# Three narrow products or one wide and one narrow: the up projection of an encoder block at near-fp32 precision

## Chip, cores and metric

The kernel runs on one NeuronCore of a Trainium2 chip. Times are device microseconds (us) of one execution. TensorE is called PE, VectorE DVE, ScalarE ACT, GpSimd POOL; SP, ACT and POOL issue the transfers (DMAs).

## What is computed

One layer of an encoder on x (512 tokens, width 2048), all in float32: RMS norm, one wide input projection feeding pooling, a short convolution and sparse attention, gates, output projection, residual. The change is in the last part, the MLP:

```python
h2 = _rmsnorm(x, norm2[l])
f = jnp.square(jax.nn.relu(jnp.einsum('bsd,df->bsf', h2, w_ff1[l])))   # 2048 -> 8192, the up stage
x = x + jnp.einsum('bsf,fd->bsd', f, w_ff2[l])                          # 8192 -> 2048, the down stage
```

## The kernel before

**Numbers.** Each float32 operand is split in a high part (type fp32r, rounded by ACT's copy) and a low part (DVE subtracts the high part from the source). A product is high x high + high x low + low x high, three passes of PE that add up in PSUM.

**Seven products.** The large matrix products are cut in two along all three dimensions and done by a scheme of seven half-size products with sums of blocks (Strassen's, in Winograd's form). The blocks of a weight are b11, b12, b21, b22; its mixes b11 + b12, b11 + b12 + b22, b12 + b22 and the sum of all four are made on DVE (`mix1`); the operand's seven parts, high and low, lie ready in `sf[h][n]` for the whole stage. The seven products n = 0 to 6 are summed into four result blocks C11, C12, C21, C22.

**The up stage.** `w_ff1` is worked through in 16 pairs (q = 0 to 15), each of 2 x 256 output columns. A pair has 14 granules: product n, half h of the contraction, in the order k = 2n + h (in pair 0 another order, `FIRST_PAIR`). A granule (`f1_granule`, L1261 on) is 4 contraction tiles j times 2 blocks m of 128 weight columns, and for each three products of 256 columns (256 tokens; the two token halves are blocks of the scheme):

```python
pe.matmul(part, hi_at(8, k)[:, cols], sh, start=first, ...)   # L1304
pe.matmul(part, hi_at(8, k)[:, cols], sl, start=False, ...)   # L1305
mm = pe.matmul(part, lo_at(8, k)[:, cols], sh, ...)           # L1306
```

One PSUM bank of 512 columns holds both m. The weight blocks are the stationary operand. ACT makes the high part of granule k (`hi1`, L1750) once granule k-4 is done, DVE the low part (`lo1`, L2612); four buffers each (`f_wh`, `f_wl`) go round. So both engines work about three granules ahead of PE, each strictly in the order in which its instructions are written: after granule k's part come that k's extras (`act_after`, `dve_after`):

- DVE, eight mixes a pair (`mix1`, L2593 to L2606, 1024 columns each), three sums of a bank with a kept copy (`add_c`, L2644 to L2648, 512 columns), and for the pair before four mixes (`mix_s`, L2656 to L2666) and seven low parts (`lo_s`, L2676) of the squared result, which the down stage will use;
- ACT, three copies of a bank (`keep`, L1769), relu and square of four blocks (`square_f`, L1783, L1785), seven high parts (`hi_s`, L1799).

Products that belong to several result blocks run in one PSUM bank as a chain, and the running sum is copied out (`keep`) before the next product is added. PE waits before h = 0 of a product for whatever last read its bank. SP loads four weight blocks a pair in two halves of 512 KB (`load_f1`) and stores the seven pieces in `f_dram` (`spill_f`), all in one queue in program order.

**Other stages.** Phases J = 0 to 5 (gates), 6 and 7 (output projection) and 8 to 15 (down stage) use products of 512 columns (L1200 to L1202). Early in the kernel POOL's queue makes tables of block sums for J = 0, 6, 7 and pair 0 in DRAM (`t_dram`): it copies a block from DRAM to DRAM and adds a second by a transfer with `accum_op`.

## Time and profile before

| | |
|---|---|
| median of 3 runs | 2651.47 us (2651.34 to 2654.2) |
| the profiled execution, its own time | 2653.83 us |
| its span, first to last instruction | 2652.0 us |
| mean granted PE clock | 0.999 of 2.4 GHz |
| busy in the span | PE 99%, PE weight loads 85%, DVE 74%, ACT 47%, POOL 4% |
| DMA over the span | 568.65 MB, mean 214 GB/s |
| up stage, products L1304 to L1306 | from 1381.4 to 2035 us |

How to read it: matmuls are pipelined and their ends are modelled, so a busy PE is not a PE at its peak, and distances between starts tell more than durations. A wait for several semaphores is put down to the one that came last. Idle time of an engine that is not the bottleneck costs nothing.

### The profile page before, as it was taken

Reading aid. Unit: us, or ns where it says so; the run is one execution under the profiler, and the core shown is the slowest. Engines: PE = TensorE matmul, PEld = TensorE weight load, DVE = VectorE, ACT = ScalarE, POOL = GpSimd, SP = SyncE. Lnnn points to the kernel's source line nnn. Section 1 sums busy time; section 2 is a strip of 40 time slices with the busy share of each in tenths; the row PEclk is TensorE's granted clock in tenths of the full one; section 3 lists DMA queues with packets and bytes.
Section 4 is the critical chain, followed back from the end, with each engine's and each line's share of the span. In section 5 each row is a group of like instructions: output and inputs, shape, how many; then the busy total and the mean of one; then the engine's idle time right before and its main releaser. Section 6 shows DMA issues by size and latency. Waiting matters only on the chain.

```text
span 2652.0 us, 36176 instructions
## 1 busy us (share of the span) xinstructions
PE 2628.2 (99%) x14130; PEld 2259.0 (85%) x14130; DVE 1953.9 (74%) x2352; ACT 1241.9 (47%) x1614; POOL 94.4 (4%) x116
## 2 busy tenths in 40 slices
PE   8999999999999999999999999999999999999999
PEld 6688877777888888888889999999999788888887
DVE  4565645567777775567668888888887988888887
ACT  6322343335444543234556656656655433333333
POOL 0022222100000000000000000000000000000000
PEclk9999999999999999999999999999999999999999
DMA  7589999946455547556764566565568777685753
GB/s 240 175 227 246 256 257 239 258 137 242 160 181 175 173 162 266 176 174 211 257 231 140 187 215 197 176 223 176 198 223 306 274 262 261 214 317 178 273 190 122
DMA packets 316804, 568.65 MB, mean 214 GB/s; under 512 B 20000, under 2 KB 128160, under 8 KB 316128
## 3 DMA queue, kind: packets, MB, share of 16 engines
q1 hardware_dynamic: 272976, 434.16, 48.5%
q0 software_dynamic: 20736, 58.73, 9.8%
q10 hardware_dynamic: 22928, 73.54, 7.5%
q8 instruction: 107, 1.75, 0.3%
q14 instruction: 57, 0.47, 0.1%
HBM read 473.95 MB, written 150.99 MB: 236 GB/s over the span
## 4 chain that ended last, share of the span: by engine, by line
PE 93%; DVE 3%; DMA 2%; issue 1%; ACT 1%; SPq 0%; ACTq 0%; DVEq 0%
PE aux L1200 8%; PE aux L1201 8%; PE aux L1202 8%; PE main L1304 8%; PE main L1306 8%; PE main L1305 8%; PE main L1200 6%; PE main L1201 6%; PE main L1202 6%; PE main L513 5%; PE main L515 5%; PE main L514 5%; PE main L1045 1%; PE main L1235 1%; PE aux L1235 1%; PE main L1047 1%
## 5 line engine op out<-in xcount | busy, mean ns | idle before, releaser
L1304 PE MATMUL main<-sf,f_wh 128*128 128x256 f32 x1728 | 489.2, 283 | 1.7 <-DVE cf_low L2737 1.4
L1305 PE MATMUL main<-sf,f_wh 128*128 128x256 f32 x1728 | 489.0, 283 | 0.0
L1306 PE MATMUL main<-sf,f_wl 128*128 128x256 f32 x1728 | 489.0, 283 | 0.0
L1304 PEld LDWEIGHTS main<-sf,f_wh 128*128 128x128 f32 x1728 | 331.8, 192 | 2.1 <-DVE cf_low L2737 1.6
L1305 PEld LDWEIGHTS main<-sf,f_wh 128*128 128x128 f32 x1728 | 331.8, 192 | 0.0
L1306 PEld LDWEIGHTS main<-sf,f_wl 128*128 128x128 f32 x1728 | 331.8, 192 | 0.0
L488 DVE TENSOR_TENSOR w_lo<-w_raw,w_hi 128x512 fp32r<-128x512 f32 (+1 forms) x184 | 123.3, 674 | 209.8 <-ACT w_hi L481 208.8
L481 ACT ACTIVATE w_hi<-w_raw 128x512 fp32r<-128x512 f32 (+1 forms) x184 | 113.4, 617 | 276.4 <-PE main L515 212.1
L513 PE MATMUL main<-act_hi,w_hi 128*128 128x512 f32 x576 | 229.7, 399 | 8.5 <-DVE w_lo L488 7.6
L1471 ACT ACTIVATE f_wh<-group 128x1024 fp32r<-128x1024 f32 x128 | 135.7, 1061 | 200.0 <-PE aux L1202 105.5
L515 PE MATMUL main<-act_hi,w_lo 128*128 128x512 f32 x576 | 225.6, 392 | 0.0
L514 PE MATMUL main<-act_lo,w_hi 128*128 128x512 f32 x576 | 225.3, 391 | 0.0
L2612 DVE TENSOR_TENSOR f_wl<-f1raw,f_wh 128x1024 fp32r<-128x1024 f32 x130 | 158.3, 1219 | 64.7 <-ACT f_wh L1750 64.7
L2149 DVE TENSOR_TENSOR f_wl<-group,f_wh 128x1024 fp32r<-128x1024 f32 x128 | 156.3, 1221 | 66.5 <-ACT f_wh L1471 66.5
L1200 PE MATMUL aux<-f_wh,sf 128*128 128x512 f32 x512 | 199.3, 389 | 2.4 <-DVE yb L2767 2.4
L1202 PE MATMUL aux<-f_wh,sf 128*128 128x512 f32 x512 | 199.2, 389 | 0.0
L1201 PE MATMUL aux<-f_wl,sf 128*128 128x512 f32 x512 | 199.2, 389 | 0.0
L1750 ACT ACTIVATE f_wh<-f1raw 128x1024 fp32r<-128x1024 f32 x130 | 136.9, 1055 | 86.2 <-PE main L1306 79.9
L1471 ACT ACTIVATE f_wh<-f2x 128x1024 fp32r<-128x1024 f32 x96 | 102.0, 1062 | 151.8 <-PE aux L1202 80.1
L2149 DVE TENSOR_TENSOR g_wl<-group_g,g_wh 128x1024 fp32r<-128x1024 f32 x80 | 97.9, 1224 | 72.8 <-ACT g_wh L1471 72.8
L1200 PE MATMUL main<-f_wh,sf 128*128 128x512 f32 x384 | 149.5, 389 | 0.5 <-DVE yb L2769 0.5
L1201 PE MATMUL main<-f_wl,sf 128*128 128x512 f32 x384 | 149.4, 389 | 0.0
(311 smaller groups left out, 5910.1 us busy)
## 6 DMA issues: line engine op xcount, KB each, us to landing
group<-w_ff SPq DMA_DIRECT2D x160, 512.0 KB, 5.1
f1raw<-w_ff SPq DMA_DIRECT2D x126, 512.0 KB, 5.6
sf<-f_dram ACTq DMA_DIRECT2D x56, 1024.0 KB, 11.2
group_g<-w_in SPq DMA_DIRECT2D x100, 512.0 KB, 4.4
w_raw<-w_in SPq DMA_DIRECT2D x87, 512.0 KB, 8.7
f_dram<-piece_hi SPq DMA_DIRECT2D x112, 256.0 KB, 4.0
f_dram<-piece_lo SPq DMA_DIRECT2D x112, 256.0 KB, 5.0
t_dram<-w_o POOLq DMA_DIRECT2D x48, 512.0 KB, 8.6
```

The source lines that it names most:

```text
L513: pe.matmul(out, wh, hi[:, kt, :], start=(kt == last_kt[0]), stop=False)
L514: pe.matmul(out, wh, lo[:, kt, :], start=False, stop=False)
L515: mm = pe.matmul(out, wl, hi[:, kt, :], start=False, stop=(kt == last_kt[1]))
L1200: pe.matmul(part, sh, wh, start=first, stop=False, skip_group_check=True)
L1201: pe.matmul(part, sh, wl, start=False, stop=False, skip_group_check=True)
L1202: mm = pe.matmul(part, sl, wh, start=False, stop=last, skip_group_check=True)
L1304: pe.matmul(part, hi_at(8, k)[:, cols], sh, start=first, stop=False, skip_group_check=True)
L1305: pe.matmul(part, hi_at(8, k)[:, cols], sl, start=False, stop=False, skip_group_check=True)
L1306: mm = pe.matmul(part, lo_at(8, k)[:, cols], sh, start=False, stop=last, skip_group_check=True)
L1471: act.activation(hi_at(J, k_of(J, n, g))[:], source_of(J, n, g).rearrange("p k c -> p (k c)"), ACT.Copy).then_inc(f_hi, 1)
L2149: dve.tensor_tensor(lo_at(J, k)[:], source_of(J, n, g).rearrange("p k c -> p (k c)"), hi_at(J, k)[:].bitcast(F32), ALU.subtract).then_inc( ...
L2612: dve.tensor_tensor(lo_at(8, k)[:], f1_source(q, n, h).rearrange("p k c -> p (k c)"), hi_at(8, k)[:].bitcast(F32), ALU.subtract).then_inc( ...
```

## The change

**Products.** In pairs 1 to 15 the high weight block is multiplied with both parts of the operand at once: a product of 512 columns, [high part | low part], into a whole bank, so that high x high lies in columns 0 to 255 and high x low in columns 256 to 511. The third product (low weight, high operand part) has 256 columns and adds to the first half. Each m has its own bank, so a product takes two banks. Pair 0 stays as it was (`f1_first`).

```diff
-                bank = main[:, (q % 2, 2, q % 2, 2, q % 2, 3, q % 2)[n], :]
+                banks = aux[:, 0:2, :] if n in (1, 3) else aux[:, 2:4, :] if n == 5 else chain_banks(q)
...
                 for j in range(4):
-                    sh, sl = sf[h][n][:, 0, j, :], sf[h][n][:, 1, j, :]
+                    both, sh = sf[h][n][:, :, j, :], sf[h][n][:, 0, j, :]
                     for m in range(2):
...
-                        pe.matmul(part, hi_at(8, k)[:, cols], sh, start=first, stop=False, skip_group_check=True)
-                        pe.matmul(part, hi_at(8, k)[:, cols], sl, start=False, stop=False, skip_group_check=True)
-                        mm = pe.matmul(part, lo_at(8, k)[:, cols], sh, start=False, stop=last, skip_group_check=True)
+                        pe.matmul(banks[:, m, :].rearrange("p (a c) -> p a c", a=2), hi_at(8, k)[:, cols], both,
+                                  start=first, stop=False, skip_group_check=True)
+                        mm = pe.matmul(banks[:, m, 0:2 * P], lo_at(8, k)[:, cols], sh, start=False, stop=last,
+                                       skip_group_check=True)
```

`chain_banks(q)` are the two `main` banks 2(q mod 2) and the next. The order of the products is now 0, 5, 2, 1, 4, 3, 6:

```diff
+        PAIR_ORDER = (0, 5, 2, 1, 4, 3, 6)
-            return 28 * 8 + 14 * q + (2 * n + h if q else FIRST_PAIR.index((n, h)))
+            return 28 * 8 + 14 * q + (2 * PAIR_ORDER.index(n) + h if q else FIRST_PAIR.index((n, h)))
```

**PE's waits before h = 0:**

```diff
+                    if n == 0:
+                            pe.wait_ge(f21_added, q - 1)
+                    if n == 5:
+                            pe.wait_ge(c_read, 3 * (q - 2) + 1)
+                    if n == 2:
+                        pe.wait_ge(kept, kept_at(q, 0))
+                    if n == 1 and q > 1:
+                        pe.wait_ge(c_read, 3 * (q - 2) + 3)
+                    if n == 4:
+                        pe.wait_ge(kept, kept_at(q, 1))
+                    if n == 3:
+                        pe.wait_ge(kept, kept_at(q, 2))
+                    if n == 6:
+                        pe.wait_ge(c_read, 3 * (q - 1) + 2)
```

**Results.** Copies of banks and the sums with them are 1024 columns wide (`kept_wide`); a fold then adds the halves. C21 is copied and added in halves (`keep_low`, `add_c21`).

```diff
+            def fold(out, wide):
+                halves = wide.rearrange("p m (a c) -> p m a c", a=2)
+                return dve.tensor_tensor(out.rearrange("p (m c) -> p m c", m=2), halves[:, :, 0], halves[:, :, 1], ALU.add)
+            def read_c11(q):
+                dve.wait_ge(g_done, k_at(q, 5, 1) + 1)
+                dve.wait_ge(kept, kept_at(q, 0))
+                dve.tensor_tensor(kept_wide[0][:], aux[:, 2:4, :], kept_wide[0][:], ALU.add).then_inc(c_read, 1)
...
+            def add_c(q, i):
+                dve.wait_ge(c_read, 3 * (q - 1) + (3, 2, 1)[i])
...
+                fold(cf[:, i, :], kept_wide[i == 0]).then_inc(c_added, 1)
+            def add_c21(q):
+                dve.wait_ge(kept, kept_at(q, 3))
+                low = cf[:, 3, :].rearrange("p (m c) -> p m c", m=2)
+                dve.tensor_tensor(low, chain_banks(q)[:, :, 0:2 * P], low, ALU.add).then_inc(f21_added, 1)
```

**Extras by k.** `HI_S_AT, LO_S_AT, MIX_S_AT = (5, 6, 7, 8, 9, 11, 13), (6, 7, 8, 9, 10, 12, 13), (6, 7, 10, 11)`. ACT: `keep(q, ...)` at k = 5, 9, 12, for the pair before `keep_low` at 2, squares at 1, 3, 4, and one of the own pair at 13. DVE: `mix1` for n = 2 at k = 3 and 4, for n = 6 at 5 and 9; for the pair before `read_c12` at 1, a fold at 2, `add_c21` at 3; `read_c11` at 8, fold 11, `read_c22` 12, fold 13. `keep` waits:

```diff
+                act.wait_ge(g_done, k_at(q, (0, 2, 1)[i], 1) + 1)
+                act.wait_ge(c_added, (3 * (q - 1) + (2 if q > 1 else 3), 3 * q, 3 * q + 1)[i])
```

**Mixes.** Two of the four mixes of a pair, b11 + b12 and b12 + b22, come from tables in DRAM (`f1t_dram`) that POOL's queue makes, 30 units of two copies and two adds of 512 KB: 14 during J = 0 to 5, 4 during the merging of the branches, 4 during J = 6 and 7, 8 at the start of pairs 1 to 8.

```diff
+            for i in range(units + 1):
+                pool.wait_ge(sum_copied, 64 * 14 + 32 * i)
+                pool.wait_ge(sum_paired, 32 * 14 + 32 * max(i - 1, 0))
...
+                elif i < units:
+                    pool.wait_ge(f_lo, k_at(i - 21, 0, 0) + 1)
+                if i < units:
+                    q, h = table_unit(i)
+                    for t in range(2):
+                        pool.dma_start(f1_table(q, t, h), f1_block(q, 0, t, h)).then_inc(sum_copied, 16)
+                if i:
+                    q, h = table_unit(i - 1)
+                    for t in range(2):
+                        pool.dma_start(f1_table(q, t, h), f1_block(q, t, 1, h), accum_op=ALU.add).then_inc(sum_paired, 16)
```

SP loads five blocks a pair instead of four, in halves. The first table goes into the buffer of b11, so its load waits for b11's low part in the same pair:

```diff
+                for h in range(2):
+                    sp.wait_ge(f_lo, k_at(q, 0, h) + 1)
+                    load_table(q, 0, h)
```

**The order on PE.** Where product n = 3 starts in a pair; `sf_3` is its operand, `sf_2` and `sf_4` those of n = 2 and 4, and `[waits ...]` names the semaphores waited for. Before:

```order
L1305 MATMUL main<-sf_2_145,f_wh_153 128x256
L1306 MATMUL main<-sf_2_145,f_wl_157 128x256
L1304 MATMUL main<-sf_3_139,f_wh_150 128x256 [waits f_lo,kept]
L1305 MATMUL main<-sf_3_139,f_wh_150 128x256
L1306 MATMUL main<-sf_3_139,f_wl_154 128x256
L1304 MATMUL main<-sf_3_139,f_wh_150 128x256
```

and now:

```order
L1357 MATMUL main<-sf_4_147,f_wh_153 128x512
L1359 MATMUL main<-sf_4_147,f_wl_157 128x256
L1357 MATMUL aux<-sf_3_139,f_wh_150 128x512 [waits f_lo,kept]
L1359 MATMUL aux<-sf_3_139,f_wl_154 128x256
L1357 MATMUL aux<-sf_3_139,f_wh_150 128x512
L1359 MATMUL aux<-sf_3_139,f_wl_154 128x256
```

Three narrow products have become a wide and a narrow one in turn. The product moved from fourth to sixth place in the pair and from a `main` to the `aux` banks; it waits for `kept` (ACT), as before, but for another copy.

**The order on DVE.** From the low part of granule 8 to that of granule 11 before:

```order
L2612 TENSOR_TENSOR f_wl_156<-f1raw_159,f_wh_152 128x1024 [waits f_hi]
L2676 TENSOR_TENSOR piece_lo_169<-cf_low,piece_hi_165 128x512 [waits s_hi]
L2612 TENSOR_TENSOR f_wl_157<-f1raw_159,f_wh_153 128x1024 [waits f_hi]
L2606 TENSOR_TENSOR f1x<-f1raw_160,f1x 128x1024 [waits f1_landed2_0,t_done,f_lo]
L2606 TENSOR_TENSOR f1x<-f1raw_160,f1x 128x1024 [waits f1_landed2_1,t_done,f_lo]
L2662 TENSOR_TENSOR cf_low<-cf_low 128x512 [waits s_lo]
L2676 TENSOR_TENSOR piece_lo_170<-cf_low,piece_hi_166 128x512 [waits s_hi]
L2612 TENSOR_TENSOR f_wl_154<-f1raw_160,f_wh_150 128x1024 [waits f_hi]
L2666 TENSOR_TENSOR cf_low<-cf_low 128x512 [waits s_lo,s_mixed]
L2612 TENSOR_TENSOR f_wl_155<-f1raw_160,f_wh_151 128x1024 [waits f_hi]
```

and now from the low part of granule 8 to the fold of C11 (L2689):

```order
L2664 TENSOR_TENSOR f_wl_156<-f1raw_159,f_wh_152 128x1024 [waits f_hi]
L2743 TENSOR_TENSOR piece_lo_174<-cf_low,piece_hi_170 128x512 [waits s_hi]
L2694 TENSOR_TENSOR kept_wide_164<-aux,kept_wide_164 128x1024 [waits kept,g_done]
L2664 TENSOR_TENSOR f_wl_157<-f1raw_159,f_wh_153 128x1024 [waits f_hi]
L2658 TENSOR_TENSOR f1x<-f1raw_160,f1x 128x1024 [waits f1_landed2_1,t_done,f_lo]
L2743 TENSOR_TENSOR piece_lo_171<-cf_low,piece_hi_167 128x512 [waits s_hi]
L2664 TENSOR_TENSOR f_wl_154<-f1raw_161,f_wh_150 128x1024 [waits f_hi]
L2743 TENSOR_TENSOR piece_lo_172<-cf_low,piece_hi_168 128x512 [waits s_hi]
L2729 TENSOR_TENSOR cf_low<-cf_low 128x512 [waits s_lo]
L2664 TENSOR_TENSOR f_wl_155<-f1raw_161,f_wh_151 128x1024 [waits f_hi]
L2733 TENSOR_TENSOR cf_low<-cf_low 128x512 [waits s_lo,s_mixed]
L2689 TENSOR_TENSOR cf_low<-kept_wide_164 128x512 [waits s_mixed,s_lo,c_read]
```

One of the two mixes has gone, the wide read of a bank and the fold have come in. L2664 is `lo1`, L2743 `lo_s`, L2729 and L2733 `mix_s`, L2658 `mix1`, L2694 `read_c11`.

**The order on ACT.** From the high part of granule 11 on:

```order
L1804 ACTIVATE f_wh_151<-f1raw_161 128x1024 [waits f1_landed3_1,g_done]
L1856 ACTIVATE piece_hi_169<-cf_low 128x512 [waits s_mixed,f_spilled2]
L1804 ACTIVATE f_wh_152<-f1x 128x1024 [waits t_done,g_done]
L1823 ACTIVATE kept_wide_164<-aux 128x1024 [waits c_added,g_done]
L1804 ACTIVATE f_wh_153<-f1x 128x1024 [waits t_done,g_done]
L1856 ACTIVATE piece_hi_170<-cf_low 128x512 [waits s_mixed,f_spilled3]
```

L1804 is `hi1`, L1856 `hi_s`. The third `keep` (L1823, from `aux`) stands behind the high part of granule 12 and waits for `c_added`, the fold above.

## Rows read from the trace of the kernel before

**Rows 1.** the page's totals: busy us (share of the span) xinstructions

```profile
PE 2628.2 (99%) x14130; PEld 2259.0 (85%) x14130; DVE 1953.9 (74%) x2352; ACT 1241.9 (47%) x1614; POOL 94.4 (4%) x116
```

**Rows 2.** the page's chain that ended last, shares of the span by engine

```profile
PE 93%; DVE 3%; DMA 2%; issue 1%; ACT 1%; SPq 0%; ACTq 0%; DVEq 0%
```

**Rows 3.** stretches: length, busy of PE, PEld, DVE, ACT, POOL (xcount); clock, DMA, GB/s

```profile
1464.00:2024.00 560.00, 560.00 (x4669) 560.00 (x4669) 474.99 (x500) 344.06 (x445) 0.00 (x0) 1.00 0.61 201
1424.00:1464.00 40.00, 39.03 (x325) 39.03 (x326) 37.61 (x48) 24.74 (x33) 0.00 (x0) 1.00 0.54 178
600.00:1040.00 440.00, 436.91 (x1920) 359.59 (x1919) 330.56 (x282) 217.81 (x230) 0.00 (x0) 1.00 0.55 187
```

**Rows 4.** timeline of PE, narrow products: start us, duration us, what

```profile
1700.81 0.28 PE L1304 MATMUL main<-sf,f_wh 128*128 128x256 f32 x1
...
1701.65 0.28 PE L1305 MATMUL main<-sf,f_wh 128*128 128x256 f32 x1
```

**Rows 5.** timeline of PE, wide products of the output projection

```profile
1303.19 0.39 PE L1202 MATMUL aux<-f_wh,smf 128*128 128x512 f32 x1
...
1305.91 0.39 PE L1202 MATMUL aux<-f_wh,smf 128*128 128x512 f32 x1
```

**Rows 6.** timeline of PE, transposes of 128 columns, start of 13

```profile
1369.32 1.59 PE L1117 MATMUL aux<-cst,mt 128*128 128x128 f32 x13
```

**Rows 7.** timeline of VectorE and ScalarE inside one pair

```profile
1631.36 0.68 DVE L2648 TENSOR_TENSOR cf_low<-main,keeps 128x512 f32<-128x512 f32 x1
1631.96 1.21 DVE L2612 TENSOR_TENSOR f_wl<-f1x,f_wh 128x1024 fp32r<-128x1024 f32 x1
...
1634.85 2.35 DVE L2598 TENSOR_TENSOR f1x<-f1raw,f1x 128x1024 f32<-128x1024 f32 x2
...
1636.16 1.06 ACT L1750 ACTIVATE f_wh<-f1x 128x1024 fp32r<-128x1024 f32 x1 [0.15 <-DVE f1x L2598]
1637.12 0.62 ACT L1799 ACTIVATE piece_hi<-cf_low 128x512 fp32r<-128x512 f32 x1
...
1645.82 1.22 DVE L2612 TENSOR_TENSOR f_wl<-f1raw,f_wh 128x1024 fp32r<-128x1024 f32 x1
1646.95 0.68 DVE L2659 TENSOR_TENSOR cf_low<-cf_low 128x512 f32<-128x512 f32 x1
1647.56 0.68 DVE L2676 TENSOR_TENSOR piece_lo<-cf_low,piece_hi 128x512 fp32r<-128x512 f32 x1
...
1645.39 0.63 ACT L1799 ACTIVATE piece_hi<-cf_low 128x512 fp32r<-128x512 f32 x1 [0.19 <-DVE cf_low L2656]
1645.93 0.58 ACT L1769 ACTIVATE keeps<-main 128x512 f32<-128x512 f32 x1
...
1649.89 1.06 ACT L1750 ACTIVATE f_wh<-f1raw 128x1024 fp32r<-128x1024 f32 x1 [1.30 <-PE main L1306]
1650.98 1.23 DVE L2612 TENSOR_TENSOR f_wl<-f1raw,f_wh 128x1024 fp32r<-128x1024 f32 x1 [1.01 <-ACT f_wh L1750]
```

**Rows 8.** what PE waited for, whole span: us in total, times, longest

```profile
PE aux L1200 <- DVE yb L2767: 2.4, 1, 2.4
PE main L1304 <- DVE cf_low L2737: 1.4, 1, 1.4
```

**Rows 9.** groups of ScalarE, pairs 1 to 15: busy us, mean ns

```profile
L1750 ACT ACTIVATE f_wh<-f1raw 128x1024 fp32r<-128x1024 f32 x112 | 118.2, 1056 | 79.8 <-PE main L1306 79.7
L1769 ACT ACTIVATE keeps<-main 128x512 f32<-128x512 f32 x42 | 24.4, 581 | 0.0
```

**Rows 10.** DMA of the up stage: a queue, and loads with us to landing

```profile
q1 hardware_dynamic: 84055, 107.53, 58.1%
f1raw<-w_ff SPq DMA_DIRECT2D x104, 512.0 KB, 5.6
```

**Rows 11.** DMA from 200 to 560 us, POOL's queue and loads beside it

```profile
q0 software_dynamic: 17037, 47.38, 60.3%
w_raw<-w_in SPq DMA_DIRECT2D x53, 512.0 KB, 10.3
```

More of the change, by code:

```diff
@@ L159, in build @@
         keeps = at("keeps", [P, 3, S], F32, 128 * KB)
+        kept_wide = [at(f"kept_wide{i}", [P, 2, S], F32, (128 + 4 * i) * KB) for i in range(2)]
         cf_low = at("cf_low", [P, 4, S], F32, 136 * KB)
@@ L1301, in f1_granule @@
                         cols = slice(j * COLS + m * P, j * COLS + (m + 1) * P)
-                        first = fresh and h == 0 and j == 0 and m == 0
+                        first = n < 6 and h == 0 and j == 0 and m == 0
                         last = h == 1 and j == 3
@@ L1315, in _ @@
             for q in range(1, F1_PAIRS):
-                for n in range(7):
+                for n in PAIR_ORDER:
                     f1_granule(q, n, 0)
@@ L1997, in _ @@
                                       ALU.mult, ALU.mult).then_inc(ws_ready, 1)
-                    dve.memset(U[:, :, 0:PADW], 0.0)
-                    dve.memset(Sa[:, :, 0:PADW], 0.0).then_inc(pads_ready, 1)
-                    dve.wait_ge(pads_ready, 1)
+                    chain.step(dve.memset(U[:, :, 0:PADW], 0.0))
+                    chain.step(dve.memset(Sa[:, :, 0:PADW], 0.0))
+                    chain.wait()
                 s = g - 3 * UP - 3
@@ L2732, in _ @@
             dve.wait_ge(kept, 3)
-            dve.tensor_tensor(keeps[:, 1, :], keeps[:, 1, :], keeps[:, 2, :], ALU.subtract).then_inc(w_added, 1)
+            chain.step(dve.tensor_tensor(keeps[:, 1, :], keeps[:, 1, :], keeps[:, 2, :], ALU.subtract))
             dve.wait_ge(g_done, k_at(0, 3, 1) + 1)
-            dve.wait_ge(w_added, 1)
+            chain.wait()
             dve.tensor_tensor(cf[:, 0, :], aux[:, 3, :], keeps[:, 1, :], ALU.add).then_inc(c_added, 1)
```

363 lines of the change are left out of this document (196 added, 167 removed).

## The prediction

> **What bounds the kernel now.** First the page's totals: TensorE (PE) is busy 2628.2 us, 99% of the span [rows 1], and the chain that ended last lies on it for 93% [rows 2]. A change pays by what it takes off TensorE, as long as nothing new makes TensorE wait. Then the stage: the stretches view shows 560 us of the up stage, some 14 of its 16 pairs, with 560.00 us of TensorE, 4669 products recorded, granted clock 1.00, VectorE (DVE) at 474.99 (85%), ScalarE (ACT) at 344.06 (61%), DMA at 0.61 [rows 3]. Of those 4669 some two lie across the window's edges: 560/4667 = 0.120 us a product. The rows give a narrow product (256 columns) 0.28 us, which is its latency: products overlap, so I take distances between starts. From 1700.81 to 1701.65 there are 7 steps: 0.120 us [rows 4]. For the wide ones (512 columns) of another stage 1303.19 to 1305.91 are 12 steps: 0.2267 us [rows 5]. The difference, 0.1067 us for 256 columns, is 0.417 ns a column, the 2.4 GHz level; so each product costs its columns plus 13.3 ns. That fixed part is what the change goes for.
>
> **Products.** Before, a block of 128 weight columns and one contraction tile takes three narrow products, 3 x 0.120 = 0.360 us; now one wide and one narrow, 0.2267 + 0.120 = 0.3467. A granule has 8 of these: 2.880 us becomes 2.773. Pairs 1 to 15 have 15 x 14 = 210 granules and lose 210 x 8 = 1680 products, as the order of PE says (13276 rows before, 11596 now): 210 x 0.1067 = **22.4 us off**. No row has the two widths in alternation. Lower bound of the gain: the wide one costs as much as two narrow ones, 0.240, gain 0. Upper bound: a product with 128 columns steps at (1.59 - 0.27)/12 = 0.110 us (13 of them in 1.59 us, the last with its own 0.27) [rows 6], so the weight swap allows little under 0.120; with 0.110 for the narrow one the gain would be 39 us. I take 22.4, since both widths show the same 13.3 ns and each keeps one weight load under one product.
> The Trainium skill (TensorE: Matmul & The Clock Gate, Back-to-back issue gap) puts the warm gap at N/2.4 + 2.5 ns. With 2.5 ns fixed the 1680 products saved would give only 4.2 us, an estimate from that page. The rows at both widths show 13.3, and they decide.
>
> **VectorE and ScalarE.** Steps, not durations, fill these engines: back to back VectorE steps 1.13 to 1.15 us for 1024 columns and 0.60 for 512 [rows 7]; a source in PSUM makes no difference (L2648 at 1631.36, the next at 1631.96). Per pair VectorE had 22 wide (14 low parts, 8 mixes) and 14 narrow (7 + 4 + 3) ones; now 21 wide (14, 4 mixes, 3 reads of the banks) and 15 narrow (7 + 4 + 3 folds + 1). By 1.15 and 0.605 that is 33.8 before (474.99 x 40.3/560 = 34.2 by the window) and 33.2 now, of a pair that shrinks from 40.3 to about 39: 85% stays 85%. ScalarE gets its three narrow copies widened and a narrow one added, 3 x 0.43 + 0.55 = 1.8: from 24.8 (344.06 x 40.3/560) to 26.6, 68%. Averages fit; the order must be followed at one place.
>
> **The new wait.** Granule 10 (n = 3, h = 0) overwrites banks that hold C12's first part, so PE waits there for the third `keep`, which ScalarE runs only after the high part of granule 12, and which waits for the fold of C11. Before, n = 3 waited for a copy that follows the high part of the next granule and was done a granule ahead; no such wait shows in the list of waits [rows 8]. I follow the chain from the end of the pair before (0 = start of granule 0):
> - last product drains and is copied low: 0.2 + 0.53 = 0.75;
> - high part 3 by ScalarE to VectorE's start, 1.10 (1649.89 to 1650.98 [rows 7]), low part 3, 1.15: 3.0;
> - mix h = 0 until ScalarE starts 1.28 (1634.85 to 1636.16 is 1.31 [rows 7]), high part 4 1.10, low part 4 1.15, mix h = 1 1.28: 7.8;
> - ScalarE: high part 5 0.97, a piece 0.53, first keep 0.97 (512 columns from a bank take 0.58 [rows 9]; with the 0.43 between 0.62 and 1.06 us of the others [rows 7, 9] I estimate about 1.0 for 1024), high part 6 1.10: 11.4;
> - VectorE from low part 6 to the fold, without a gap: 8 wide and 10 narrow, 9.2 + 6.05, and 0.13 for a dependent one: 26.8 (the order on DVE in the section on the change shows the last 12 of these 18);
> - third keep until PE may start 1.10: 27.9 to 28.0.
> PE wants it at 10 x 2.773 = 27.7. So it is **late by about 0.25 us a pair: +3.8 us**. Bounds: 0 if steps are 1% shorter; 2.0 us a pair if each instruction takes its full duration (1.22, 0.68, 1.06) instead of its step.
> What queues behind: the high part of 13 stands behind that keep, but PE needs it 8 us later. The other new waits have room: the first keep is done by 10.4, where PE is due for granule 4 at 11.1; the second by 19.8 against 22.2; the reads of C22 and C12 are two to four granules ahead.
>
> **Transfers.** SP loads ten 512 KB blocks a pair instead of eight: 3.0 us of all engines per MB (107.53 MB in 58.1% of 560 us [rows 10]), +3.2 us, DMA share 0.61 to 0.71. The tables cost 120 transfers on POOL's queue; such ones took 60.3% of 360 us for 47.38 MB, 90 of 0.524 MB, so 2.4 us each [rows 11]. 22 of 30 units fall before the up stage, where the share is 0.55 [rows 3] and PE's list of waits names no DMA (its two longest entries of the later stages are [rows 8]): I cost them at nothing; what covers them is the ring of three groups that SP loads ahead, and if that failed each unit could cost its 9.6 us at most. Eight units fall into pairs 1 to 8, 9.6 us of all engines each: share (24.6 + 3.2 + 9.6)/39.1 = 0.96 there. The transfer that matters is the first table: issued after low part 0 at -5.7, needed by the mix at 3.0, 8.7 us for a landing that takes 5.6 [rows 10]. I take 0; the upper bound is the landing beside POOL's traffic, 10.3 [rows 11], 1.6 us late in eight pairs.
>
> **Ends.** In pair 1 the first table can be loaded only within the pair, with VectorE busiest (37.61 of 40 before [rows 3]); in the down stage VectorE gets 1.15 + 0.6 more in the first three granules, where PE already waits 2.4 once [rows 8]. Bounds 0 to 7; I take **+1.5**, nearer to 0, since PE waits only 1.4 us there before [rows 8].
>
> **Sum.** -22.4 + 3.8 + 1.5 = -17.1. The profiled execution took 2653.8 (span 2652.0); it would take 2636.7. Its time is 2.4 above the median shown, 2651.5, so the forecast by the median is **2634.3**.
>
> **Rivals.**
> - The chain fits after all and the ends cost nothing: 2651.5 - 22.4 = 2629. Speaks for it: it misses by 0.25 in 28. Chance 0.10.
> - Tables late: 1.6 us in pairs 1 to 8, +12.8: 2647. For: share 0.96. Against: POOL's four transfers are over before the next load is urgent. 0.13.
> - No gain from width, because products of unequal width pay at each change: granule 2.88 again, the chain then has 28.8 us and fits, 2651.5 + 1.5 = 2653. Against: the fixed part is equal at both widths. 0.08. The Trainium skill (TensorE: Matmul & The Clock Gate, Back-to-back issue gap) with its fixed 2.5 ns would end near there, at an estimated 2651.5 - 4.2 + 1.5 = 2649.
> - Slower: the wait at granule 10 at 2.0 us a pair, +30 - 22.4 + 1.5: 2660. It turns the sign from 1.4 us a pair ((22.4 - 1.5)/15). For: VectorE has no slack between low part 6 and the fold, and each 1% on it is 0.15 us. Against: the steps in [rows 7]. 0.09.
> That the change does less than it says is excluded by the order's counts.
>
> **Numbers.** Forecast case 0.60, own range 2631 to 2640. The whole range 2627 to 2652 holds it, the fitting chain and the late tables, and leaves out the slower case and most of the third rival. Faster by over 0.2% (about what can be told from no change) means under 2646.2: 0.60 + 0.10 + half of 0.13 = 0.76; within it 0.13; slower 0.11.
>
> **What would show it.** A PE timeline that steps 0.227 and 0.120 in turn; 27.7 us of granules 0 to 9 and then a gap of 0.1 to 0.5 us once a pair, put down to ScalarE's `kept_wide` copy from `aux`; pair starts 39.1 apart; VectorE near 85%. Steps of 0.24 would prove the third rival, gaps above 1.4 us the fourth, VectorE waiting for `f1raw` in pairs 1 to 8 alone the second. I am wrong if PE's gaps lie elsewhere.

## The result and the profile after

The changed kernel takes 2678.77 us (median of 4, 2678.25 to 2679.63), the one before beside it 2652.47. The ratio is 1.0098 [1.0085, 1.011] (the brackets, here and below, hold the 95% interval), 1% **slower**, clear of the noise. The forecast was 2634.3 with a range of 2627 to 2652: both sign and range are wrong. The profiled execution took 2679.63 us, its span is 2677.9.

The page's totals and its chain that ended last, after:

```profile
PE 2627.1 (98%) x12450; PEld 2173.5 (81%) x12450; DVE 1947.2 (73%) x2352; ACT 1263.3 (47%) x1629; POOL 210.6 (8%) x236
...
PE 82%; DVE 7%; DMA 6%; ACT 2%; issue 2%; SPq 1%; ACTq 0%; DVEq 0%
```

PE has 1680 products fewer than in [rows 1], yet its busy time fell by 1.1 us only, and the chain lies on PE for 82% where it was 93% [rows 2]. DVE and transfers took that share. The granted clock, below, says why the busy time hardly fell. What PE waited for, whole span, after (us in total, times, longest):

```profile
PE main L1357 <- ACT kept_wide L1823: 8.3, 9, 2.0
PE main L533 <- DVE w_lo L508: 7.6, 2, 7.4
PE aux L1357 <- ACT kept_wide L1823: 7.5, 8, 2.3
PE main L1270 <- DVE b_lo L2442: 6.8, 1, 6.8
PE aux L1235 <- DVE kept_wide L2704: 4.6, 1, 4.6
```

The second row stood in the profile before as well. The first and third are waits for ScalarE's keeps in the up stage, 17 of them, before granules 4, 8 and 10. The fourth lies outside the change: the start of the merge, the stage ahead of phase 6. The last is the start of the down stage. The keeps were late because ScalarE, which makes them, stood still before them. It waited for the spills, the stores of the pieces, and DVE for the load of a table; from 1464 to 2024 us the wait for spills was 1.1 us before, and there were no tables to load:

```profile
ACT piece_hi L1856 <- DMA f_dram<-piece_lo: 25.2, 11, 4.1
...
DVE f1x L2653 <- DMA f1raw<-f1t_dram: 9.6, 6, 3.1
```

Each of PE's 17 waits can be followed back through the semaphores, from what ended it to what that had waited for. Within 16 us 11 of them (10.5 us) lead to the landing of a spill and 3 (4.3 us) to that of a table's load; 3 small ones (1.0 us) lead to neither.

Where the 25.9 us between the two profiled spans came from. The parts are cut at the first product of pair 1 (L1304 before, L1357 after) and at the last one of that line in pair 15; the wait ahead of the down stage is in the last part:

| part | before | after | lost |
|---|---|---|---|
| start to pair 1 | 1430.8 | 1443.3 | +12.5 |
| pairs 1 to 15 | 604.5 | 614.7 | +10.2 |
| the rest | 616.7 | 619.9 | +3.2 |

Half of the loss lies **before the first changed product**, where the 22 units of table transfers are new. The stretches view of the merge's start, before (length, busy of PE, PEld, DVE, ACT, POOL, clock, DMA, GB/s):

```profile
1010.00:1020.00 10.00, 10.00 (x46) 8.29 (x45) 6.57 (x6) 3.36 (x5) 0.00 (x0) 1.00 0.06 22
1020.00:1030.00 10.00, 10.00 (x46) 8.29 (x45) 7.97 (x8) 6.26 (x7) 0.00 (x0) 1.00 0.89 318
1030.00:1040.00 10.00, 10.00 (x46) 8.28 (x45) 4.81 (x5) 2.81 (x4) 0.00 (x0) 1.00 1.05 365
```

and after:

```profile
1010.00:1020.00 10.00, 10.00 (x46) 8.29 (x45) 7.04 (x6) 3.54 (x4) 1.51 (x2) 1.00 0.62 222
...
1030.00:1040.00 10.00, 10.00 (x46) 8.29 (x45) 5.00 (x5) 4.80 (x7) 0.18 (x1) 1.00 1.10 335
1040.00:1050.00 10.00, 10.00 (x46) 8.29 (x45) 4.35 (x5) 4.33 (x7) 1.33 (x2) 1.00 1.03 366
1050.00:1060.00 10.00, 10.00 (x45) 8.27 (x45) 1.99 (x3) 2.31 (x4) 1.17 (x1) 1.00 1.09 352
```

A DMA share near 1.05 is a full set of engines. Before, the stage's average of 0.55 [rows 3] was made of stretches at 0.06 and others at 1.05. After, the merge's first loads share a full stretch that lasts to 1060 us, and PE waits 6.8 us for them.

A wait can cost more than its length. At six waits of PE of 1.8 to 6.8 us (one at phase 0, at the merge's start, in pair 0, in pairs 9 and 15 and at the down stage's start) the granted clock stands at 0.50, the lower level of 1.2 GHz, for some 24 us in all. Before, it does so at one wait of 1.8 us, in pair 0, for 3.4 us, and not at the one of 2.4 us [rows 8]. Two equal stretches after the wait of 4.6 us:

```profile
2063.10:2066.50 3.40, 3.40 (x8) 2.72 (x9) 3.40 (x4) 2.05 (x3) 0.00 (x0) 0.50 0.99 355
2066.50:2069.90 3.40, 3.40 (x16) 2.79 (x16) 3.35 (x4) 2.84 (x5) 0.00 (x0) 1.00 1.03 416
```

PE is busy for all of both, and makes 8 products in the one and 16 in the other. In the first, products of 512 columns step at 0.43 us and not at 0.227, some 1.6 us lost in 8 products. For the five stretches that are new this is an estimated 7 to 8 of the 25.9 us, and most of what the 1680 products saved in busy time.

In the up stage, the start of products in an undisturbed pair, timeline of PE after:

```profile
1859.69 0.40 PE L1357 MATMUL main<-sf,f_wh 128*128 128x512 f32 x1
1859.93 0.28 PE L1359 MATMUL main<-sf,f_wl 128*128 128x256 f32 x1
1860.04 0.40 PE L1357 MATMUL main<-sf,f_wh 128*128 128x512 f32 x1
1860.27 0.28 PE L1359 MATMUL main<-sf,f_wl 128*128 128x256 f32 x1
1860.39 0.40 PE L1357 MATMUL main<-sf,f_wh 128*128 128x512 f32 x1
...
1861.81 0.40 PE L1357 MATMUL aux<-sf,f_wh 128*128 128x512 f32 x1
```

Six wide and six narrow products lie between 1859.69 and 1861.81: 0.3533 us for one of each, where 0.3467 was forecast. The steps after a wide product are 0.23 and 0.24, those after a narrow one 0.11 and 0.12 (from 1855 to 1930 us 0.236 and 0.117 in the mean). Pairs 10 to 14 took 39.2 to 39.6 us each, 40.3 before; pairs 1 to 9 took 39.7 to 42.9, pair 15 took 44.9.

### The profile page after: what moved, and what is told of

It is laid out like the page before. It is cut to its first block, busy times and chain, and to the rows that moved or that the text cites. A ratio compares the mean times of both kernels' runs of the same rounds, so it can differ in the third digit from the quotient of the medians.

```text
span 2677.9 us, 32985 instructions
## 1 busy us (share of the span) xinstructions
PE 2627.1 (98%) x12450; PEld 2173.5 (81%) x12450; DVE 1947.2 (73%) x2352; ACT 1263.3 (47%) x1629; POOL 210.6 (8%) x236
## 3 DMA queue, kind: packets, MB, share of 16 engines
q0 software_dynamic: 61056, 121.65, 21.5%
## 4 chain that ended last, share of the span: by engine, by line
PE 82%; DVE 7%; DMA 6%; ACT 2%; issue 2%; SPq 1%; ACTq 0%; DVEq 0%
PE aux L1235 8%; PE aux L1236 8%; PE aux L1237 8%; PE main L1235 6%; PE main L1237 6%; PE main L1236 6%; PE main L533 5%; PE main L535 5%; PE main L534 5%; PE main L1357 4%; PE aux L1357 3%; DMA f_dram<-piece_lo 2%; PE main L1359 2%; DMA f1raw<-f1t_dram 2%; DVE f_wl L2664 2%
## 5 line engine op out<-in xcount | busy, mean ns | idle before, releaser
L1357 PE MATMUL main<-sf,f_wh 128*128 128x512 f32 x960 | 342.3, 400 | 8.3 <-ACT kept_wide L1823 8.3
L1359 PE MATMUL main<-sf,f_wl 128*128 128x256 f32 x960 | 269.7, 281 | 0.0
L1357 PE MATMUL aux<-sf,f_wh 128*128 128x512 f32 x720 | 257.8, 400 | 7.6 <-ACT kept_wide L1823 7.5
L2664 DVE TENSOR_TENSOR f_wl<-f1raw,f_wh 128x1024 fp32r<-128x1024 f32 x160 | 195.3, 1221 | 76.5 <-ACT f_wh L1804 76.0
L1357 PEld LDWEIGHTS main<-sf,f_wh 128*128 128x128 f32 x960 | 180.9, 188 | 55.2 <-ACT kept_wide L1823 11.5
L1804 ACT ACTIVATE f_wh<-f1raw 128x1024 fp32r<-128x1024 f32 x160 | 168.1, 1056 | 88.3 <-PE aux L1359 44.0
L1359 PE MATMUL aux<-sf,f_wl 128*128 128x256 f32 x720 | 202.5, 281 | 0.0
L1359 PEld LDWEIGHTS main<-sf,f_wl 128*128 128x128 f32 x960 | 182.0, 190 | 0.0
L1357 PEld LDWEIGHTS aux<-sf,f_wh 128*128 128x128 f32 x720 | 135.9, 189 | 43.5 <-ACT kept_wide L1823 10.7
## 6 DMA issues: line engine op xcount, KB each, us to landing
sf<-f_dram ACTq DMA_DIRECT2D x56, 1024.0 KB, 11.6
```

Source lines behind the costliest of these rows:

```text
L1357: pe.matmul(banks[:, m, :].rearrange("p (a c) -> p a c", a=2), hi_at(8, k)[:, cols], both, start=first, stop=False, skip_group_check=True)
L1359: mm = pe.matmul(banks[:, m, 0:2 * P], lo_at(8, k)[:, cols], sh, start=False, stop=last, skip_group_check=True)
L1804: act.activation(hi_at(8, k)[:], f1_source(q, n, h).rearrange("p k c -> p (k c)"), ACT.Copy).then_inc(f_hi, 1)
L2664: dve.tensor_tensor(lo_at(8, k)[:], f1_source(q, n, h).rearrange("p k c -> p (k c)"), hi_at(8, k)[:].bitcast(F32), ALU.subtract).then_inc( ...
```

## The experiments

Two theories at first. **A:** the wide product gives half of what was forecast, and the 120 table transfers cost the rest by landing beside urgent ones. **B:** the new arrangement of banks and keeps is too tight by itself. Medians stand below; before was measured beside each batch, at 2652.7 to 2653.5 us.

**x1: no tables.** The POOL loop is gone, and `load_table` loads a plain block of `w_ff` in its place. So the two mixes are left out of the result, here and in x4, x6, x9 and x10.

```diff
-                sp.wait_ge(sum_paired, table_at(q, h))
-                sp.dma_start(f1raw[i][:, h], f1_table(q, i, h)).then_inc(f1_landed[i][h], 16)
+                sp.dma_start(f1raw[i][:, h], f1_block(q, 0, 1, h)).then_inc(f1_landed[i][h], 16)
```

> The changed kernel with POOL's 120 table transfers left out; SP loads a plain block of the weight, as large, in place of each table (so products n = 1, 2, 4, 6 of pairs 1 to 15 get wrong sums of blocks). Theory A, the table transfers crowd the DMA engines: the 2.5 us lost at the start of J = 0, 9.4 in the merging stage and 16.4 in pairs 1 to 9 go away, about 28 us, so about 2650 us with pairs 1 to 9 at 39.6 us like pairs 10 to 14 now; pair 15 (44.9) keeps its loss. Theory B, the order on ScalarE and VectorE and SP's ten loads make the waits: PE still waits for kept_wide in pairs 1 to 9, over 2665 us.

Measured: 2650.17 us, ratio 0.9991 [0.9982, 1.0001]. 28.6 us off the changed kernel, which is more than the whole loss. PE's waits for keeps are 3.9 us in 4 (15.8 in 17 in the change), ScalarE's waits for spills 6.1 us (25.2). Theory A holds.

**x2: the kernel before, with the table transfers.** The same loop on POOL is added to the old kernel, and nobody reads the tables.

> The kernel before with the change's 120 table transfers added on POOL's queue; nobody reads the tables. Theory A: slower by about 12 us before the up stage (2.5 at the start of J = 0, 9.4 in the merging stage), 2664 us; in the up stage little or nothing, since the old order has more room between pieces and kept copies, so that crowding alone is not enough there. Theory B: within 3 us of 2652.

Measured: 2666.36 us, 1.0049 [1.0032, 1.0065]. So 13 us are the price of traffic alone, and all of it lies before pair 1, which starts at 1443.8 us (1430.8 before). What PE waited for in it:

```profile
PE main L1243 <- DVE b_lo L2390: 8.1, 1, 8.1
```

Its up stage lost nothing with the same 8 units in it: each pair takes 40.3 us, as before. The stretches view of it:

```profile
1464.00:1790.00 326.00, 326.00 (x2719) 326.00 (x2718) 276.06 (x295) 198.61 (x262) 29.42 (x30) 1.00 0.87 249
```

PE is busy for all of it at a DMA share of 0.87. In the changed kernel this stretch has 0.86, and PE busy for 313.93 of 326. So in the up stage it is the new arrangement **and** the traffic together. (To the new arrangement belong SP's two more loads a pair: this stretch moves 249 GB/s here and 267 in the changed kernel.) The Trainium skill (DMA: Bandwidth & Descriptors, Issuing engines are not separate DMA queues) says transfers "interleave with each other, regardless of the engine that started them"; the wait of 8.1 us, caused by POOL's queue on SP's loads, agrees.

**x3: the keeps first.** On ScalarE, the keeps of granules 5, 9 and 12 go ahead of the pieces' high parts that may wait for a spill.

```diff
-                if k - late in HI_S_AT:
-                    hi_s(q - 1, HI_S_AT.index(k - late))
                 if q < F1_PAIRS and k in (5, 9, 12):
                     keep(q, (5, 9, 12).index(k))
+                if k - late in HI_S_AT:
+                    hi_s(q - 1, HI_S_AT.index(k - late))
```

(The third keep also goes ahead of `hi1` of granule 12.)

> The changed kernel with the three bank copies of a pair put ahead of the piece's high part (k = 5, 9) and of the high part of granule 12 on ScalarE. If late stores of the pieces, on which ScalarE waits ahead of the copies, are what turns crowding into PE's waits, the waits before granule 8 go and most of pair 15's: 5 to 12 us off, 2667 to 2674. If VectorE's lateness alone makes them, nothing changes beyond 2 us. If the order were all (theory B), 16 us or more off.

Measured: 2678.58 us, ratio 1.0101, the change's own time. Nothing is gained, as in the expectation's second outcome, but not for its cause, VectorE alone. PE waits for keeps less often, 10 times, but 13.8 us in all, and the longest is one of 4.5 us before granule 4:

```profile
PE main L1357 <- ACT kept_wide L1823: 6.0, 2, 4.5
```

Followed back, both waits of this row end at a table's load, which took 9.6 and 11.5 us to land. Of the eight waits before granule 10 six still end at a spill: the first two keeps stand ahead of the piece now, but the steps that lead to the fold, and so to the third keep, still stand behind it. From 1440 to 1790 us ScalarE waited 33.3 us for spills, 25.1 in the change.

**x4: wide, wide, narrow, narrow.** As x1, and each j issues its two wide products first, then its two narrow ones.

```diff
                     for m in range(2):
                         cols = slice(j * COLS + m * P, j * COLS + (m + 1) * P)
                         pe.matmul(banks[:, m, :].rearrange("p (a c) -> p a c", a=2), hi_at(8, k)[:, cols], both,
                                   start=first, stop=False, skip_group_check=True)
+                    for m in range(2):
+                        cols = slice(j * COLS + m * P, j * COLS + (m + 1) * P)
                         mm = pe.matmul(banks[:, m, 0:2 * P], lo_at(8, k)[:, cols], sh, start=False, stop=last,
                                        skip_group_check=True)
```

> As x1_no_tables (table transfers left out, same wrong sums), with the products of a contraction tile in the order wide, wide, narrow, narrow instead of wide, narrow, wide, narrow. If the extra time of a wide product in alternation (0.240 instead of 0.227 us in most granules) comes from loading its weights under a narrow product, only one of two wide products pays it: granules near 2.80 instead of 2.83 us, 5 us less than x1_no_tables. If it comes with the product's own form (two runs of 256 columns from the operand), granules stay at 2.83 us and the time equals that of x1_no_tables within 2 us.

Measured: 2644.39 us, 0.9967 [0.9954, 0.9979], 5.8 less than x1. Its timeline of PE (a row with x2 holds two products):

```profile
1860.20 0.63 PE L1356 MATMUL main<-sf,f_wh 128*128 128x512 f32 x2
1860.66 0.40 PE L1360 MATMUL main<-sf,f_wl 128*128 128x256 f32 x2
1860.90 0.63 PE L1356 MATMUL main<-sf,f_wh 128*128 128x512 f32 x2
...
1862.29 0.63 PE L1356 MATMUL main<-sf,f_wh 128*128 128x512 f32 x2
```

From 1860.20 to 1862.29 are three rounds of 0.697 us, 0.3483 for one of each: most of the missing 0.0067 is back.

**x9: the wide product split.** As x1, but the wide product is two of 256 columns, in the same place and into the same banks.

```diff
-                        pe.matmul(banks[:, m, :].rearrange("p (a c) -> p a c", a=2), hi_at(8, k)[:, cols], both,
-                                  start=first, stop=False, skip_group_check=True)
+                        for a in range(2):
+                            pe.matmul(banks[:, m, a * 2 * P:(a + 1) * 2 * P], hi_at(8, k)[:, cols], both[:, a, :],
+                                      start=first, stop=False, skip_group_check=True)
```

> The kernel of x1_no_tables with one edit: the wide product is issued as two narrow ones of 256 columns, one for each half of the operand, into the same banks and in the same place (the table transfers stay out, so the two mixes of the tables are left out of the result). Everything else of the new arrangement stays. If the width is worth what the granules show (39.58 us a pair against 40.32), each granule goes back to 2.880 us and the kernel takes 2650.2 + 210 x (2.880 - 2.827) = about 2661 us. If it was the new order of keeps and buffers that gave or took the time and not the width, it stays within 2 us of 2650.

Measured: 2662.19 us, 1.0029 [1.0017, 1.004]: 12.0 more than x1 (10 by the two ratios, each to the kernel before in its own batch). **That is the worth of the width**, 11 forecast from the steps.

**x10: tables unread.** The changed kernel with all 120 transfers, but SP loads plain blocks without waiting for a table.

> The changed kernel with all 120 table transfers as they are, but nothing reads the tables: the up stage loads plain blocks of w_ff in their place, at once, without the wait for the table's transfers (the two mixes are left out of the result). If the up stage loses by the traffic, which makes all landings late, it stays at about 2677 us. If it loses because a table is late when its half is wanted (VectorE waited 9.6 us in all for f1raw<-f1t_dram), pairs 1 to 9 fall back towards 39.6 us and it is about 2665 us.

Measured: 2676.95 us, 1.0093 [1.0076, 1.011]. The traffic does it, and not a table that is made too late. It does not exclude a load that lands late, since SP still loads as much at the same points. In its profiled execution the 15 pairs took 607.1 us against 614.7, the medians differ by 1.8; up to that much may be the wait for a table.

**x5: tables at other points.** Only when POOL may issue the units before the up stage is changed.

```diff
                 if i < 14:
-                    pool.wait_ge(f_lo, 12 * i + 4)
+                    pool.wait_ge(f_lo, 28 + 10 * i)
                 elif i < 18:
-                    pool.wait_ge(lo_ready, u_b + 16 * (i - 14) + 1)
+                    pool.wait_ge(lo_ready, u_b + 10 * (i - 14) + 24)
```

> The changed kernel with the same 120 table transfers, but the ones before the up stage released at other points of the program (not just ahead of the first loads of the token columns and of the merge). If the 12 us lost before pair 0 come from single transfers that happen to stand in front of urgent loads, they come back: about 2666 us, with pair 0 starting at about 1382 to 1384 us. If they come from the sheer traffic, the loss only moves to other places: 2676 to 2680 us.

Measured: 2669.17 us, 1.006 [1.0043, 1.0077]: 9.6 off. Pair 1 starts at 1432.8 (1443.3 in the change), and the wait at the merge is 1.2 us. The same bytes at other times cost 2.0 us before pair 1 in place of 12.5.

**x6: an earlier read.** As x4, and DVE's second read of C12 of pair 15 stands one granule earlier (`read_c12` at k = 0 of phase 8).

> The kernel of x4_two_by_two (no table transfers, products in the order wide, wide, narrow, narrow; the mixes of the tables' two operands are left out, plain blocks take their place), and beside it the last read of the second keep in pair 15 stands one granule earlier on VectorE's and ScalarE's lists. If the 4.6 us that TensorE waits at the start of the down stage come from that read standing behind a high part that waits for the end of pair 15: about 2640 us. If the wait only passes to the next buffer: 2644 us as x4_two_by_two.

Measured: 2645.82 us, 0.9972 [0.9961, 0.9984], x4's time. **A miss:** the wait for `kept_wide` of 4.6 us is gone, and another came 30 us later (1.2 us in x4):

```profile
PE aux L1234 <- DVE yb L2845: 4.2, 1, 4.2
```

From 2000 to 2060 us its DMA share is 0.99 to 1.03. The edit only moved the wait. That transfers bound the start of the down stage is likely by that share, but no run tested it.

**x7: one table, and x8: all tables.** x8 has the whole change with the edits of x4, x5 and x6. x7 is x8 with one of the two tables' mixes made on DVE again, two more additions a pair and its blocks loaded at other points, and has 60 transfers less.

> All of the change with all table transfers, plus the three edits found so far: tables released at other points (x5), products wide, wide, narrow, narrow (x4), the last read earlier (x6). If the three are independent: 2678.6 - 12 - 6 - 4.5 = about 2656 us. If the table transfers of the up stage set its pace by themselves, the order of the products gives nothing there and it is about 2662 us.

> As x8, but only one of the two mixes comes as a table (60 transfers by GpSimd in place of 120); the other is made on VectorE again from the two blocks, 28 additions of 1.22 us more. If the up stage loses by the traffic, about 16 us with 120 transfers, half of it comes back: 2656 - 8 = about 2648 us, faster than the kernel before by 4. If VectorE, busy 530 of 617 us in these pairs before the 34 us more, becomes the bound: 2660 us or more.

Measured: x8 2666.64 us, 1.0051 [1.0034, 1.0068]; x7 2677.89 us, 1.0095 [1.0078, 1.0112]. In x7 PE waits for ScalarE's keeps 31 times, also in pairs without any table traffic:

```profile
PE main L1359 <- ACT kept_wide L1827: 17.1, 16, 1.8
PE aux L1359 <- ACT kept_wide L1827: 9.8, 15, 2.9
```

From 1830 to 2000 us, where no unit runs, PE waits for them 9 times (never in x8), and DVE is busy 149.0 of 170 us. DVE had become the bound, as the rival in the expectation said. x8 is slower than its sum by 10: its pairs took 611.5 us against 591.5 in x4, which has no tables. Its trace shows how. ScalarE in x8, the second half of a pair:

```profile
1530.28 1.06 ACT L1806 ACTIVATE f_wh<-f1raw 128x1024 fp32r<-128x1024 f32 x1 [1.20 <-PE main L1361]
1534.75 0.63 ACT L1858 ACTIVATE piece_hi<-cf_low 128x512 fp32r<-128x512 f32 x1 [3.41 <-DMA f_dram<-piece_lo]
1535.29 1.00 ACT L1825 ACTIVATE kept_wide<-main 128x1024 f32<-128x1024 f32 x1
```

A piece's buffer comes free when its spill has landed; that is 3.4 us late, the keep stands behind it, and PE waits 0.53 us, until 1536.35, for the keep. The same delay goes on through the low part and the fold to the third keep, for which PE waits 1.02 us at 1543.2. Over 1440 to 1780 us ScalarE waited for that:

```profile
ACT piece_hi L1858 <- DMA f_dram<-piece_lo: 24.4, 9, 3.9
```

against 1.2 us in x4. And POOL's issues in x8 (L2989 the two copies of a unit, L2993 an accumulation):

```profile
1508.15 1.52 POOL L2989 DMA_DIRECT2D f1t_dram<-w_ff  x2 [22.68 <-DVE f_wl L2666]
1519.06 1.20 POOL L2993 DMA_DIRECT2D f1t_dram<-w_ff  x1 [9.39 <-issue]
1525.71 1.17 POOL L2993 DMA_DIRECT2D f1t_dram<-w_ff  x1 [5.46 <-issue]
```

The unit starts at 1508, its last transfer is issued at 1525.7 and lands 10.9 us later: 28 us in all; the units before and after it take 24 and 25. Now the same 20 us in x4, without tables:

```profile
1512.00:1517.00 5.00, 5.00 (x31) 4.38 (x30) 4.41 (x5) 3.05 (x5) 0.00 (x0) 1.00 0.00 0
1517.00:1522.00 5.00, 5.00 (x30) 4.35 (x29) 3.79 (x4) 4.28 (x6) 0.00 (x0) 1.00 0.00 0
1522.00:1527.00 5.00, 5.00 (x30) 4.37 (x29) 4.89 (x7) 2.87 (x5) 0.00 (x0) 1.00 0.62 162
1527.00:1532.00 5.00, 5.00 (x31) 4.33 (x29) 5.00 (x7) 3.46 (x4) 0.00 (x0) 1.00 1.07 351
```

A pair's own transfers fill the engines for some 22 us and leave them empty for 10. In x8 the stretch 1527 to 1532 holds the last accumulation:

```profile
1527.00:1532.00 5.00, 5.00 (x30) 4.34 (x30) 5.00 (x7) 2.65 (x3) 0.00 (x0) 1.00 0.98 141
```

The share is nearly the same, the bytes are 141 GB/s against 351. (This pair starts 3.4 us later in x8 than in x4, so a part of the missing bytes was only due later.) That gave the last theory: the loss is not the sum of the traffic, but its **overlap with full stretches**.

**x11: all units before the up stage.** 20 units in phases 0 to 5, 5 in the merge, 5 in phases 6 and 7. The products are in x4's order.

> The whole change, products in the order of x4, and the release of the table transfers changed so that all 30 units are over before the up stage: 20 in the first six token columns (14 before), 5 in the merge, 5 in the two columns behind it. If the 8 units in pairs 1 to 8 are what costs the 16 us there, the up stage runs as in x4 (592 us against 616 us); if the transfers before it still find room at a DMA share of 0.79 to 0.86, the kernel takes 2669 - 16 - 6 = about 2648 us. If that room is gone, the loss comes back before the up stage: 2658 us or more.

Measured: 2662.59 us, 1.0033 [1.0019, 1.0047]. The pairs take 591.6 us, as in x4, and pair 1 starts at 1446.8: the loss has moved, as its second case said.

**x12: in the gaps.** With x4's order and x6's earlier read, as x13 and x14 too. 24 units before, the six others cut in two: copies at the start of one pair, accumulations at the start of the next.

```diff
+                if i < 15:
+                    pool.wait_ge(f_lo, 24 + 9 * i)
+                elif i < 19:
+                    pool.wait_ge(lo_ready, u_b + 10 * (i - 15) + 24)
+                elif i < 24:
+                    pool.wait_ge(f_lo, 28 * 6 + 11 * (i - 19) + 4)
+                elif i < units:
+                    pool.wait_ge(f_lo, k_at(1 + 2 * (i - 24), 0, 0) + 3)
                 if i < units:
...
+                if i >= 24:
+                    pool.wait_ge(f_lo, k_at(2 + 2 * (i - 24) - i // units, 0, 0) + 3)
                 if i:
```

> The whole change with the edits of x8, and the table transfers of the up stage put where a pair has no other traffic. The trace of x4_two_by_two shows a DMA share of 1.04 to 1.07 over some 22 us of each pair and of 0.00 over its first 10; in x8 the four transfers of a unit start in the last of the full stretch and take about 24 us, so that the last of them lies in the next full stretch (1527 to 1532 us: share 0.98, but 141 GB/s). Here a unit is cut in two: its two copies at the start of one pair, its two accumulations at the start of the next, six units in pairs 1 to 13, the other 24 before the up stage. If the loss there comes from that overlap, the 15 pairs take 592 to 598 us against 612 in x8, and the kernel 2650 to 2653 us. If it comes from the sum of the traffic, six units in place of eight leave three quarters of the 20 us: about 2662 us.

Measured: 2655.87 us (11 runs, 2650.96 to 2659.56), 1.0011 [1.0002, 1.0021]. The pairs take 592.2 us with six units in them, and between 1490 and 1970 us PE waits for nothing. The total missed its case by 3 us: pair 1 starts at 1437.1, since phases 6 and 7 with five units reach a DMA share of 1.00 and PE waits 3.3 us there.

**x13 and x14: dealt out anew.** x13: 16 units in phases 0 to 5, 4 in the merge, 3 in phases 6 and 7, 7 in the gaps of the pairs. x14: 15, 5, 3 and 7.

> As x12_in_gaps, whose 15 pairs ran in 592 us, with the units of the stages before the up stage dealt out anew: 16 in the first six token columns, 4 in the merge, 3 in the two columns behind it (15, 4 and 5 in x12, where TensorE waited 3.3 us and pair 1 started at 1437.1 us, against 1430.5 with 4 units there in x8), and 7 in the empty stretches of pairs 0 to 14 (6 in x12). If the rest of the loss comes from the transfers in columns 6 and 7, where the DMA share was 0.90 to 1.00, pair 1 starts at about 1431 us and the kernel takes 2648 to 2650 us, faster than before (2653) by 0.1 to 0.2%. If a table of pairs 14 and 15 now comes too late, or the seventh unit collides with the first pair's loads, it stays at 2655 us or more.

> As x13_gaps_and_seven, where columns 6 and 7 lost nothing, but TensorE waited 5.8 us at the start of the merge: a unit took about 29 us there, so 16 of them did not fit in the 462 us of the first six columns, and the last ran at 1031 to 1061 us, beside the merge's first loads. Here 15 units lie in the columns (as in x12, wait 0.7 us) and 5 in the merge, which begin at its loads' 16th turn. If the wait at the merge's start is that one unit's, pair 1 starts at about 1431 us and the kernel takes about 2649 us, under before's 2653. If the fifth unit in the merge costs as much there as the sixteenth did ahead of it, 2654 us as x13.

```diff
-                if i < 16:
-                    pool.wait_ge(f_lo, 26 + 44 * i // 5)
+                if i < 15:
+                    pool.wait_ge(f_lo, 24 + 9 * i)
                 elif i < 20:
-                    pool.wait_ge(lo_ready, u_b + 10 * (i - 16) + 24)
+                    pool.wait_ge(lo_ready, u_b + 10 * (i - 15) + 16)
```

Measured: x13 2654.86 us (11 runs), 1.001 [1.0001, 1.0019]: phases 6 and 7 ran without a wait, but PE waited 5.8 us at the merge's start, so pair 1 began at 1437.4 again. The time is that of the expectation's second outcome (2655 or more), by a third cause. x14 **2647.12 us** (11 runs, 2643.77 to 2651.49), 0.9978 [0.9969, 0.9987]. It contains the whole change with all 120 table transfers and is 0.2% faster than the kernel before, 1.2% faster than the change as made. It is the sixth placement of the units, the change's own included. Its pairs take 591.3 us with seven units in them. Its first and last wide products in `main`, and what is left of waits in the up stage:

```profile
L1357 PE MATMUL main<-sf,f_wh x960: 389/396/501, 1432.1 to 2023.4; 128*128 128x512 f32 x192
```

```profile
PE aux L1357 <- ACT kept_wide L1825: 2.8, 2, 2.3
...
PE main L1357 <- ACT kept_wide L1825: 2.0, 2, 1.3
```

Its queue of table transfers moved the same 121.65 MB as the change's. Without tables this kernel is x6, at 2645.82 us. So in this place the 120 transfers cost 1.3 us (1.6 by the ratios), where the change paid 28.6 for them: the traffic itself is nearly free, and its place made the loss.

## Why the prediction was wrong

By the terms of its sum:

- **Products, -22.4: mis-sized, -11 to -12 measured.** The step "no row has the two widths in alternation" took 0.2267 for the wide product, the value from a stream of wide ones [rows 5]. Between narrow ones it steps at 0.236 (its lower bound was 0.240), and the narrow after it at 0.117: 0.3533 for both, 0.74 us a pair, 11.1 in 15 pairs; x9 measured 10 to 12. At some times, as after a wait, the granules were the forecast 2.773 us, at others 2.827. Why they settle on the slower was not found; x4's order avoids most of it. The Trainium skill (TensorE: Matmul & The Clock Gate, Back-to-back issue gap) with 2.5 ns of fixed cost would have given an estimated 4.2 us; x9's 12.0 lies between that and the forecast, and the trace's 0.3533 against 0.360 decides.
- **New wait at granule 10, +3.8: rightly worked out, but 0 in most undisturbed pairs.** With granules of 2.827 PE wants the bank at 28.3, and the chain ends at 27.9 to 28.0. The pairs of 39.6 us show none of it (14 x 2.827 = 39.58). Where granules did take 2.773 us, it is there: in x1's pair 2 granule 9 starts at 1495.26, 10 at 1498.11 and 11 at 1500.99, 0.18 us more than two such granules, where 0.25 was forecast. But the chain is as tight as worked out, and that made it the place where late transfers show: the waits before granules 4, 8 and 10 are keeps.
- **Transfers, 0: the step that failed; +28.6 measured (x1).** "22 of 30 units fall before the up stage, where the share is 0.55: I cost them at nothing" read an average, and named as cover SP's ring of groups. The stretches within that average stood at 0.06 and at 1.05, and the ring was no cover at the merge's start, whose first loads came 6.8 us late. In the pairs, "POOL's four transfers are over before the next load is urgent" took 9.6 us of engine time for the unit's length; its four transfers take 24 us or more one after another, into the next full stretch. The working named 9.6 us a unit as the upper bound, and carried none of it to the range: 22 units at a mere 0.6 us are the 13 us found. The sum also had no term for the clock, which fell at waits and took an estimated 7 to 8 us; most of that lies in the 28.6, the rest in the ends.
- **Ends, +1.5: 9 measured** in x1, 2 above its upper bound of 7: 1.1 in pair 1, 3.3 in pair 15 (39.6 against 42.9), 4.7 in the down stage, where the DMA share is 0.99 to 1.03 (in x6).
- **The sum with what was measured:** -11.6 for the products, 0 for granule 10, 9 for the ends and 28.6 for the transfers are +26.0, where the medians differ by 26.3.
- **Rivals.** "Tables late" was right in its mechanism for the smaller part: loads of tables landed in 9.2 us from 1464 to 1790 us (the median; its bound had 10.3), DVE waited 9.6 us for them, and 4.3 of PE's 15.8 us go back to them. The larger part, 10.5 us, goes back to spills, which the rival did not name, and it said nothing of the 12.5 us before pair 1. "No gain from width" was half true. The slower rival named one of the right places, granule 10, and the wrong cause: engine steps, where it was late landings. VectorE was forecast near 85% and read 83% (463.27 of 560 us).

Not settled: why the old arrangement stands the same traffic in the up stage without a loss (x2). That its keeps have more slack is the likely reason, but only argued: x3 changed only their order, and x2 also lacks SP's two more loads a pair.

## What to carry to other kernels

A DMA share averaged over a stage says nothing of room: cut it into stretches of 5 to 10 us, lay the length of the added transfers (issue to last landing, not their engine time) over the full and the empty ones, and release them at the start of an empty one. Price extra traffic by whose landing it delays (spills that free a buffer, the first loads of a stage), and give it a term above zero wherever a stretch is full. A wait of PE may cost more than its length: at six of them in the change the lower clock took an estimated 1.5 us more each. A step measured in a uniform stream is a bound, not a value, for a mixed one.

## What the runs showed of the hardware

- A 512-column product with its own weight load steps at 0.227 us among its like and at 0.236 between 256-column ones, which then step at 0.117 and not at 0.120; two and two in turn cost 0.3483 for one of each, one and one 0.3533, and three of 256 columns 0.360.
- The granted clock fell to 0.50 at each of the six waits of PE of 1.8 to 6.8 us after the change that are told above, but not at waits of 2.4 us in the kernel before and 2.3 us in x14; products of 512 columns then stepped at 0.43 us.
- Transfers that accumulate from DRAM into DRAM hold the engines at a low throughput. In x8 the part of a pair that is empty in x4 (0.00) reads as follows. The first accumulation is issued at 1559.77, behind the unit's copies, and has the second row nearly to itself:

```profile
1557.00:1562.00 5.00, 5.00 (x30) 4.35 (x29) 3.44 (x4) 2.59 (x4) 1.17 (x1) 1.00 0.24 59
1562.00:1567.00 5.00, 4.91 (x29) 4.13 (x28) 3.79 (x5) 3.70 (x6) 0.47 (x1) 1.00 0.66 99
```

  A share of 0.66 moves 99 GB/s there, where the pair's own transfers move 351 at 1.07.
- Executions of x12, x13 and x14 lie within 8.6, 4.6 and 7.7 us over 11 runs each, those of the kernel before beside them within 3.1 to 3.7 over 15. x1 without tables has 5.0 over 10, so the traffic is not shown to be the cause.
